# One encoder layer on one core: the softmax denominators turned into columns, the first loads reordered, the last norm taken into the feed-forward stage

## The chip, the cores and the metric

One core of one Trainium2 chip. The metric is the device time of one launch in microseconds; the median of the runs of the kernel before is 2854.69 us (2854.2 to 2859.28, three runs).

## What is computed

A transformer-like layer on two sequences of 512 and 1024 tokens (1536 tokens, twelve tiles of 128), model width 1024, all in float32:

```python
h = rmsnorm(x, norm_mix_pre); z = h @ w_in
a_out = axial_gqa(aq, ak, av, q_norm, k_norm) @ w_attn_o     # 8 query heads, 2 key heads, head width 64
m_out = bidir_mlstm(mq, mk, mv, mo, gates, ...) @ w_mlstm_o  # 4 heads of 128, both directions
x = x + rmsnorm((sigmoid(ga) * a_out + sigmoid(gm) * m_out) @ w_out, norm_mix_post)
u = rmsnorm(x, norm_ffn_pre) @ w_up
y = (gelu(conv3(u[..., :2816])) * u[..., 2816:]) @ w_down
return x + rmsnorm(y, norm_ffn_post)
```

In the attention the scores of a head are exp(q.k - top), the probabilities are weighted with v, and the result is divided by the sum of the probabilities. q and k are normed per head with one gain of 64 numbers for queries and one for keys.

## The kernel before, in words

Every product is made of three float32r products (high and low parts of both operands, `mm3`, L75). The engines' programs are written out by hand, each engine runs its list in order, and they meet at semaphores. The stages follow each other behind barriers: `norm_and_qkv`, `attention`, `mlstm`, `mlstm_norm`, `merge`, `out_projection`, `ffn`, `final_norm`.

**`norm_and_qkv`**, for each of twelve tiles of tokens: ScalarE takes the squares and the root (`statistics`), VectorE scales (`scale`), TensorE turns (`turn_x`), both keep high and low parts (`keep_hi`, `keep_lo`), TensorE projects (`project`). The weights come in eight slices of 128 x 784; VectorE makes the high part and the low part of each (`split_w`: a cast, L268, and a subtraction, L270). `raw` holds four slices, so slice 4 is asked for when slice 0 is split. Before ScalarE takes its first square it issues, on its own queue, the load of `mix_gain`, ten loads of head gains (one for each of the ten heads, a row of 64 numbers sent to 128 partitions) and the tables `cos` and `sin`.

**`attention`** works on 24 units: a key head, a chunk of 512 queries, a query head. A unit has 4 or 8 tiles of keys and takes 2 or 4 steps, 80 steps in all, each step two tiles of keys. The engines run over slots, one step each, with the work of several steps in one slot: at slot i TensorE does a part of the projection that fills the gaps (`project`, 384 units of three matmuls), `turn_top` of the unit that starts at slot i+3, `weigh(i)`, more of the projection, `scores(i+2)`, `sums` of the unit that ended at slot i-1, and the `piece`s. ScalarE does `exp(i+1)` and `keep_hi(i+1)`, VectorE `keep_lo(i+1)`, then `invert` and `normalise`, `fold`, the projection's low parts, `reduce` of the pieces, `top` and `add_halves`. GpSimd adds up the probabilities (`p_sum`, L723).

A `piece` is a 128 x 512 block of scores, made only for its row maximum; VectorE reduces it out of PSUM (`pM`, two banks). `turn_top` turns the four columns of maxima into a row in PSUM (`pD`, one bank, L944), and ScalarE copies it beside the queries (`keep_top`). `sums` multiplies a 128 x 128 matrix of ones with the folded probabilities, so that all 128 rows of the same bank `pD` hold the 512 denominators (L976, L977); `invert` takes the reciprocal of 64 x 512 of them into `att_rinv` (L842), and `normalise` multiplies (L849). Because `pD` is used by both, TensorE's program waits in front of `turn_top`:

```python
                for u in starting(i + 3):
                    if sums_done:
                        pe.wait_ge(inverted, sums_done)
                    turn_top(u)
```

**`ffn`** goes over 22 blocks of 128 hidden units. For each block TensorE makes the gate (`pG`) and the value (`pVal`), ScalarE and VectorE the convolution, the gelu and the split activation (`activate`), TensorE twelve tiles x two halves of the down projection, and VectorE adds each half to `y_sum` (`add_down`, L2072). The last block's `down_products` waits for all three chunks of the activation.

**`final_norm`** is a stage of its own: for each tile ScalarE takes the squares and the root, VectorE the reciprocal, the scaled product (L2245) and the sum with `x1` (L2250), SyncE stores the tile.

Of the kernel before, what the change touches and what calls it, by code (L numbers as in the profile page):

```python
# [30 lines left out]
P = 128  # L31
D = 1024
# [49 lines left out]
def norm_and_qkv(nc, k):  # L82

    with ExitStack() as ctx:
# [14 lines left out]
        qk_gain = sb("qk_gain", [P, NHEADS_QK, HEAD])  # L99
        cos = sb("cos", [P, NT, HEAD // 2])  # L100
# [44 lines left out]
        def _(sp):  # L145
# [30 lines left out]
            for kt in range(1, 4):  # L176
                load_w(kt)
            load_x(2)
# [17 lines left out]
        def _(act):  # L196
# [68 lines left out]
        def _(dve):  # L265
            def split_w(kt):
                dve.wait_ge(w_in[kt % 4], 32 * (kt // 4 + 1))
                dve.tensor_copy(wq_hi[:, kt, :], raw[:, kt % 4, :]).then_inc(w_hi_done, 1)  # L268
# [45 lines left out]
            split_w(0)  # L314
            dve.wait_ge(gain_in, 16)
            scale(0)
            split_w(1)
            scale(1)
            split_w(2)
            keep_lo(0)  # L320
# [5 lines left out]
            dve.wait_ge(const_in, 16 * (NHEADS_QK + 2))  # L326

            dve.tensor_scalar(qk_gain[:, 0:NQ, :], qk_gain[:, 0:NQ, :], Q_SCALE, None, ALU.mult).then_inc(gain_scaled, 1)
            dve.wait_ge(gain_scaled, 1)
# [11 lines left out]
        def _(pool):  # L341
            pool.wait_ge(const_in, 16 * (NHEADS_QK + 2))
# [182 lines left out]
def attention(nc, k):  # L525

    with ExitStack() as ctx:
# [35 lines left out]
        ones = sb("att_ones", [P, P], F32R)  # L563
# [4 lines left out]
        o_half, o_sum, o_out = sb("o_half", [H2, CH]), sb("o_sum", [H2, CH]), sb("o_out", [H2, 2, CH])  # L568
        top2, tops = sb("att_top2", [P, 4, 2]), sb("att_tops", [P, 4, P])
        rinv = sb("att_rinv", [H2, CH])  # L570
# [4 lines left out]
        g_ones = sb("gate_ones", [R, 2 * CH])  # L575
# [14 lines left out]
        summed, inverted, normed = sem("p_summed"), sem("inverted"), sem("o_normed")  # L590
# [24 lines left out]
        def pieces_until(i):  # L615
            return sum(len(x) for x in PIECES[:i + LEAD])

# [7 lines left out]
        def _(sp):  # L625
# [47 lines left out]
            for i in slots():  # L673
# [14 lines left out]
                for u in ending(i - 2):  # L688
# [37 lines left out]
        def _(act):  # L726
# [14 lines left out]
            def keep_top(u):  # L741
                act.wait_ge(m_turned, u + 1)
                act.wait_ge(q_in[u % 3], 48 * (u // 3 + 1))
                act.activation(q_m[H2:H2 + 1, u % 3, :], pD[H2:H2 + 1, :], ACT.Copy).then_inc(m_kept, 1)
# [50 lines left out]
        def _(dve):  # L795
            def reduce(u, p):
# [4 lines left out]
                if n == 1:  # L801
                    if u and p == 0:
                        dve.wait_ge(m_turned, u)
                    dve.tensor_reduce(tops[:, qb, H2:H2 + 1], pM[:, at % 2, :], AX_X, ALU.max).then_inc(reduced, 1)
                else:
                    dve.tensor_reduce(top2[:, qb, s:s + 1], pM[:, at % 2, :], AX_X, ALU.max).then_inc(reduced, 1)  # L806
# [25 lines left out]
            def add_halves(u):  # L832
                dve.wait_ge(halved, u + 1)
                if u:
                    dve.wait_ge(normed, u)
                dve.tensor_tensor(o_sum[:, :], pO[0:H2, :], o_half[:, :], ALU.add).then_inc(o_added, 1)

            def invert(u):
                dve.wait_ge(summed, u + 1)
                if u:  # L840
                    dve.wait_ge(normed, u)
                dve.reciprocal(rinv[:, :], pD[0:H2, :]).then_inc(inverted, 1)  # L842

            def normalise(u):
                dve.wait_ge(inverted, u + 1)
# [3 lines left out]
                dve.tensor_tensor(o_out[:, u % 2, :], o_sum[:, :], rinv[:, :], ALU.mult).then_inc(normed, 1)  # L849
# [1538 lines left out]
```

## Time and profile before

| | us |
|---|---|
| median of three runs (lowest, highest) | 2854.69 (2854.2, 2859.28) |
| profiled execution, its own time | 2859.45 |
| span of the profile, first to last instruction | 2857.6 |
| TensorE busy | 2483.2 (87%) |
| VectorE busy | 1786.3 (63%) |
| ScalarE busy | 885.8 (31%) |
| GpSimd busy | 497.1 (17%) |

The profile is of one execution. The shares are means over stages: by the turn of the attention's first piece at 199.1 us, of its last sums at 852.7 us, of the feed-forward stage's first product at 1729.1 us and its last sum's start at 2813.1 us, each stage has to be read by itself. Matmuls are pipelined: a 128 x 512 matmul is listed with 0.39 us, and the next starts 0.23 us after it.

### The profile page before, as it was taken

The numbers are of one execution on the slowest core, as the hardware profiler recorded it, in microseconds if no ns is written. First come the engines' busy times: TensorE is split into PE (matmuls) and PEld (weight loads), VectorE is DVE, ScalarE is ACT, GpSimd is POOL, SyncE is SP. The second block draws the span as 40 slices with busy tenths as digits, with TensorE's granted clock in tenths as the row PEclk, the third lists the DMA queues.
The fourth block names the chain that finished last, engine by engine and source line by source line (L and its number), as shares of the span: only waits on it lengthen the run. The fifth ranks groups of instructions, "written<-read, shape, count | busy, mean of one in ns | idle before, by whom it ended". The sixth has DMA issues, their size and how long they took to land. (4 is left out here: it accounts for less than half of the span.)

```text
span 2857.6 us, 32937 instructions
## 1 busy us (share of the span) xinstructions
PE 2483.2 (87%) x11024; PEld 2034.7 (71%) x11024; DVE 1786.3 (63%) x2308; ACT 885.8 (31%) x1395; POOL 497.1 (17%) x430
## 2 busy tenths in 40 slices
PE   5948778878886999997597988999999999999993
PEld 4836666657664878876485776888888888888882
DVE  4626777777764666665534553757576666656577
ACT  2314434434443554544410331111212111111113
POOL 1521222222323544443221000000000000000000
PEclk9968889989997999998798998999999999999996
DMA  6774224323217454532354431111101011111104
GB/s 179 200 195 119 80 70 132 104 69 116 81 54 223 115 177 116 158 96 88 128 182 147 138 116 52 38 29 35 31 22 42 24 37 29 37 29 37 29 15 184
DMA packets 286224, 268.20 MB, mean 94 GB/s; under 512 B 21672, under 2 KB 228776, under 8 KB 286128
## 3 DMA queue, kind: packets, MB, share of 16 engines
q1 hardware_dynamic: 281376, 253.18, 29.7%
q10 hardware_dynamic: 4752, 13.83, 1.2%
q8 instruction: 49, 0.80, 0.1%
q14 instruction: 47, 0.39, 0.0%
HBM read 197.70 MB, written 69.26 MB: 93 GB/s over the span
## 5 line engine op out<-in xcount | busy, mean ns | idle before, releaser
L2072 DVE TENSOR_TENSOR y_sum<-y_sum,pVal 128x512 f32<-128x512 f32 x252 | 171.5, 687 | 208.6 <-PE pVal L79 208.6
L77 PE MATMUL pG<-h2T_hi,wg_hi 128*128 128x512 f32 x528 | 206.5, 391 | 11.2 <-DVE wg_lo L2019 11.2
L78 PE MATMUL pG<-h2T_hi,wg_lo 128*128 128x512 f32 x528 | 206.3, 391 | 0.0
L79 PE MATMUL pG<-h2T_lo,wg_hi 128*128 128x512 f32 x528 | 206.3, 391 | 0.0
L77 PE MATMUL pVal<-h2T_hi,wv_hi 128*128 128x512 f32 x528 | 205.4, 389 | 0.0
L78 PE MATMUL pVal<-h2T_hi,wv_lo 128*128 128x512 f32 x528 | 205.4, 389 | 0.0
L79 PE MATMUL pVal<-h2T_lo,wv_hi 128*128 128x512 f32 x528 | 205.4, 389 | 0.0
L723 POOL TENSOR_TENSOR p_sum<-p_sum,probs 128x1024 f32<-128x1024 f32 x56 | 137.0, 2446 | 379.9 <-ACT probs L733 379.9
L1201 POOL TENSOR_TENSOR w_sum<-w_sum,w_all 128x512 f32<-128x512 f32 (+3 forms) x128 | 149.5, 1168 | 240.9 <-DVE w_all L1306 219.2
L77 PE MATMUL pZ_a<-hT_hi_a,win_hi_a 128*128 128x512 f32 x384 | 158.0, 412 | 31.5 <-DVE win_lo_a L497 27.6
L2117 ACT ACT_TABLE_LOAD x22 | 28.2, 1283 | 477.1 <-DVE conv L2052 477.1
L2072 DVE TENSOR_TENSOR y_sum<-y_sum,pD 128x512 f32<-128x512 f32 x252 | 172.3, 687 | 0.6 <-PE pD L79 0.6
L77 PE MATMUL pZ_m<-hT_hi_m,win_hi_m 128*128 128x512 f32 x384 | 159.4, 415 | 6.6 <-DVE win_lo_m L497 6.3
L78 PE MATMUL pZ_a<-hT_hi_a,win_lo_a 128*128 128x512 f32 x384 | 156.5, 407 | 0.0
L79 PE MATMUL pZ_a<-hT_lo_a,win_hi_a 128*128 128x512 f32 x384 | 155.5, 405 | 0.0
L78 PE MATMUL pZ_m<-hT_hi_m,win_lo_m 128*128 128x512 f32 x384 | 154.3, 402 | 0.0
L79 PE MATMUL pZ_m<-hT_lo_m,win_hi_m 128*128 128x512 f32 x384 | 153.9, 401 | 0.0
L806 DVE TENSOR_REDUCE att_top<-pM 128x1 f32<-128x512 f32 x128 | 86.7, 689 | 96.5 <-PE pM L938 96.5
L819 DVE TENSOR_TENSOR p_lo<-probs,p_hi 128x1024 fp32r<-128x1024 f32 x80 | 130.6, 1632 | 10.7 <-ACT p_hi L739 9.7
L733 ACT ACTIVATE probs<-pS 128x512 f32<-128x512 f32 x160 | 87.5, 595 | 156.3 <-PE pS L956 156.2
L497 DVE TENSOR_TENSOR win_lo_m<-win_raw_m,win_hi_m 128x1024 fp32r<-128x1024 f32 x48 | 67.5, 1406 | 97.4 <-ACT win_hi_m L493 97.4
L77 PEld LDWEIGHTS pG<-h2T_hi,wg_hi 128*128 128x128 f32 x528 | 99.8, 189 | 32.4 <-DVE wg_lo L2019 11.6
(260 smaller groups left out, 6272.4 us busy)
## 6 DMA issues: line engine op xcount, KB each, us to landing
win_raw_a<-in_w_in SPq DMA_DIRECT2D x48, 512.0 KB, 4.2
win_raw_m<-in_w_in SPq DMA_DIRECT2D x48, 512.0 KB, 4.2
ffn_raw<-in_w_up SPq DMA_DIRECT2D x44, 512.0 KB, 3.9
zT_scratch<-z_st_a SPq DMA_DIRECT2D x48, 256.0 KB, 4.4
zT_scratch<-z_st_m SPq DMA_DIRECT2D x48, 256.0 KB, 4.4
a_T<-zT_scratch SPq DMA_DIRECT2D x16, 768.0 KB, 8.6
ffn_raw<-in_w_down SPq DMA_DIRECT2D x22, 512.0 KB, 4.4
m_raw<-zT_scratch SPq DMA_DIRECT2D x36, 256.0 KB, 3.1
```

The lines of the kernel that those rows point to most:

```text
L77: pe.matmul(out, w_hi, x_hi, start=first, stop=False, **kw)
L78: pe.matmul(out, w_lo, x_hi, start=False, stop=False, **kw)
L79: return pe.matmul(out, w_hi, x_lo, start=False, stop=last, **kw)
L497: dve.tensor_tensor(self.w_lo[:, g % 2], self.raw[:, g % 2], self.w_hi[:, g % 2].bitcast(F32), ALU.subtract).then_inc(self.split, 1)
L723: pool.tensor_tensor(acc[:, u % 2, :], acc[:, u % 2, :], probs[:, i % 2, :], ALU.add).then_inc(added_up, 1)
L733: act.activation(probs[:, i % 2, a * CH:(a + 1) * CH], pS[:, a, :], ACT.Exp).then_inc(exped, 1)
L806: dve.tensor_reduce(top2[:, qb, s:s + 1], pM[:, at % 2, :], AX_X, ALU.max).then_inc(reduced, 1)
L819: dve.tensor_tensor(p_lo[:, i % 3, :], probs[:, i % 2, :], p_hi[:, i % 3, :].bitcast(F32), ALU.subtract).then_inc(lo_done, 1)
L1201: pool.tensor_tensor(w_sum[:, j % 2, d, cols], w_sum[:, j % 2, d, cols], w_all[:, x % RING, cols], ALU.add).then_inc(added_up, 1)
L2072: dve.tensor_tensor(y_sum[:, t, cols], y_sum[:, t, cols], down_bank(2 * t + h), ALU.add).then_inc(summed, 1)
L2117: act.activation(gelu[:, :], conv[:, :], ACT.Gelu_apprx_tanh, bias=b).then_inc(gelu_done, 1)
```

## The change

Three parts.

**Start.** The ten loads of head gains on ScalarE's queue become two (`head_gain`), and they, `cos` and `sin` go on SyncE's queue behind the first four weight slices; VectorE spreads the two gains over ten heads. The high parts of the weights are made by ScalarE (`w_high`) between its squares, VectorE keeps the subtraction.

**Attention.** The maxima are turned into a bank of `pM`, which they share with the pieces in the order `M_ORDER`; `wait_bank` waits for whoever held the bank two places before. `sums` takes the folded probabilities as the weights and two columns of ones as the moving side, four blocks x (high, low), so that the denominators of 128 queries stand in a column. `invert` takes the reciprocal of 128 x 4 and spreads it to 128 x 512 by a product with ones (`rwide`); `turn_inverse` turns that back into rows of `pD`; `normalise` multiplies straight out of `pD`. Each of these has a slot of its own: `sums` at one slot after the unit's end, `invert` and `turn_inverse` at two, `normalise` and the store at three. `o_sum` has two buffers.

**End.** `final_norm` goes; in `ffn` the last block's down projection goes tile by tile through two pairs of banks and starts with the first chunk of the activation, VectorE adds a whole tile at once (`last_sum`), ScalarE takes the squares, VectorE scales two tiles later (`scale`), GpSimd adds `x1`, SyncE stores. `x1` is loaded into the place of `h2_hi` during the last block's value products.

```diff
@@ norm_and_qkv
+            sp.dma_start(cos[:, :, :], k.cos).then_inc(const_in, 16)
+            sp.dma_start(sin[:, :, :], k.sin).then_inc(const_in, 16)
+            for g, src in enumerate((k.q_norm, k.k_norm)):
+                sp.dma_start(head_gain[:, g, :], src.partition_broadcast(P)).then_inc(const_in, 16)
             load_x(2)
...
+            def w_high(kt):
+                act.wait_ge(w_in[kt % 4], 32 * (kt // 4 + 1))
+                act.activation(wq_hi[:, kt, :], raw[:, kt % 4, :], ACT.Copy).then_inc(w_hi_done, 1)
...
-            for h in range(NHEADS_QK):
-                g = k.q_norm if h < NQ else k.k_norm
-                act.dma_start(qk_gain[:, h, :], g.partition_broadcast(P)).then_inc(const_in, 16)
-            act.dma_start(cos[:, :, :], k.cos).then_inc(const_in, 16)
-            act.dma_start(sin[:, :, :], k.sin).then_inc(const_in, 16)
             statistics(0)
+            w_high(0)
             statistics(1)
+            w_high(1)
             keep_hi(0)
+            w_high(2)
+            w_high(3)
             keep_hi(1)
+            for kt in range(4, KD):
+                w_high(kt)
@@ attention
+        def wait_bank(pe, m):
+
+            if m >= 2:
+                kind, n = M_ORDER[m - 2]
+                pe.wait_ge(m_kept if kind == "turn" else reduced, n + 1)
...
             def invert(u):
                 dve.wait_ge(summed, u + 1)
+                dve.reciprocal(rinv[:, :], pD[:, 0:8].rearrange("p (q e) -> p q e", e=2)[:, :, 0]).then_inc(inverted, 1)
+                dve.wait_ge(inverted, u + 1)
                 if u:
-                    dve.wait_ge(normed, u)
-                dve.reciprocal(rinv[:, :], pD[0:H2, :]).then_inc(inverted, 1)
+                    dve.wait_ge(r_turned, u)
+                dve.tensor_tensor(rwide[:, :, :], wide_ones, rinv[:, :].unsqueeze(2).to_broadcast([P, 4, P]),
+                                  ALU.mult).then_inc(widened, 1)
...
-                dve.tensor_tensor(o_out[:, u % 2, :], o_sum[:, :], rinv[:, :], ALU.mult).then_inc(normed, 1)
+                dve.tensor_tensor(o_out[:, u % 2, :], o_sum[:, u % 2, :], pD[0:H2, :], ALU.mult).then_inc(normed, 1)
...
             def sums(u):
                 pe.wait_ge(fold_split, u + 1)
-                pe.matmul(pD[:, :], ones[:, :], s_hi[:, :], start=True, stop=False)
-                pe.matmul(pD[:, :], ones[:, :], s_lo[:, :], start=False, stop=True).then_inc(summed, 1)
+                if u:
+                    pe.wait_ge(normed, u)
+                for qb in range(4):
+                    cols = slice(qb * P, (qb + 1) * P)
+                    pe.matmul(pD[:, 2 * qb:2 * qb + 2], s_hi[:, cols], ones[:, :], start=True, stop=False)
+                    last = pe.matmul(pD[:, 2 * qb:2 * qb + 2], s_lo[:, cols], ones[:, :], start=False, stop=True)
+                last.then_inc(summed, 1)
+
+            def turn_inverse(u):
+                pe.wait_ge(widened, u + 1)
+                for qb in range(4):
+                    last = pe.transpose(pD[:, qb * P:(qb + 1) * P], rwide[:, qb, :], k.ident[:, :])
+                last.then_inc(r_turned, 1)
...
                 for u in starting(i + 3):
-                    if sums_done:
-                        pe.wait_ge(inverted, sums_done)
                     turn_top(u)
...
                 for u in ending(i - 1):
-                    pe.wait_ge(m_kept, tops_done)
                     sums(u)
-                    sums_done += 1
+                for u in ending(i - 2):
+                    turn_inverse(u)
@@ ffn
+                pool.tensor_tensor(row, row, x_row(t), ALU.add).then_inc(added, 1)
...
+            dve.wait_ge(post_in, 16)
+            for t in range(NT + 2):
+                if t < NT:
+                    last_sum(t)
+                if t >= 2:
+                    scale(t - 2)
...
-            down_products(last_f)
...
+                pe.wait_ge(act_l, NCH * last_f + t // 4 + 2)
+                if t >= 2:
+                    pe.wait_ge(done_t, t - 1)
```

## Rows read from the trace of the kernel before

**Rows 1.** Busy time of all engines in the attention: PE, PEld, DVE, ACT, POOL, PEclk, DMA.

```profile
216.00:853.00 637.00, 519.52 (x2074) 411.00 (x2072) 469.97 (x452) 280.15 (x390) 161.90 (x80) 0.90 0.32 92
```

**Rows 2.** Waits within the attention, 216 to 853 us: total, times, longest.

```profile
PE pDen L944 <- DVE att_rinv L842: 89.6, 20, 6.9
...
PE pO L969 <- DVE o_sum L836: 11.0, 6, 5.4
```

**Rows 3.** VectorE's groups over the span: busy, mean ns | idle before.

```profile
L842 DVE RECIPROCAL att_rinv<-pDen 64x512 f32<-64x512 f32 x24 | 80.2, 3342 | 0.5 <-PE pDen L977 0.5
...
L830 DVE TENSOR_TENSOR p_fold_lo<-p_fold,p_fold_hi 128x512 fp32r<-128x512 f32 x24 | 16.6, 692 | 0.8
```

**Rows 4.** VectorE in order of time, around one of these waits: start, us.

```profile
504.72 0.85 DVE L815 TENSOR_TENSOR att_tops<-att_top 128x4 f32<-128x4 f32 x1
...
508.30 3.34 DVE L842 RECIPROCAL att_rinv<-pDen 64x512 f32<-64x512 f32 x1
```

**Rows 5.** TensorE in order of time, behind the same wait.

```profile
511.69 1.11 PE L944 MATMUL pDen<-ident,att_tops 128*128 128x128 f32 x4 [6.35 <-DVE att_rinv L842]
...
513.46 0.63 PE L969 MATMUL pO<-p_hi,v_both 128*128 128x512 f32 x1
513.88 0.63 PE L970 MATMUL pO<-p_lo,v_both 128*128 128x512 f32 x1
...
515.90 0.39 PE L956 MATMUL pS<-q_max,k_low 65*128 65x512 f32 x1
516.13 0.39 PE L955 MATMUL pS<-q_stack,k_stack 128*128 128x512 f32 x1
```

**Rows 6.** TensorE in order of time: eight transposes in the first stage.

```profile
44.96 1.03 PE L374 MATMUL pT<-ident,x_scaled 128*128 128x128 f32 x8
```

**Rows 7.** TensorE in order of time: sixteen two-column matmuls of the mLSTM stage.

```profile
920.53 0.25 PE L1439 MATMUL pMV<-m_ones,w_sum_lo 128*128 128x2 f32 x1
920.64 0.25 PE L1438 MATMUL pMV<-m_ones,w_sum_hi 128*128 128x2 f32 x1
...
922.01 0.35 PE L1438 MATMUL pMV<-m_ones,w_sum_hi 128*128 128x2 f32 x1
922.23 0.35 PE L1439 MATMUL pMV<-m_ones,w_sum_lo 128*128 128x2 f32 x1
```

**Rows 8.** GpSimd in order of time, two of its sums.

```profile
517.58 2.40 POOL L723 TENSOR_TENSOR p_sum<-p_sum,probs 128x1024 f32<-128x1024 f32 x1 [12.04 <-ACT probs L733]
...
527.90 2.62 POOL L723 TENSOR_TENSOR p_sum<-p_sum,probs 128x1024 f32<-128x1024 f32 x1 [3.82 <-ACT probs L733]
```

**Rows 9.** VectorE in order of time, beside these sums.

```profile
518.63 2.44 DVE L819 TENSOR_TENSOR p_lo<-probs,p_hi 128x1024 fp32r<-128x1024 f32 x1 [0.21 <-ACT p_hi L739]
...
524.10 1.23 DVE L819 TENSOR_TENSOR p_lo<-probs,p_hi 128x1024 fp32r<-128x1024 f32 x1 [0.19 <-ACT p_hi L739]
...
528.77 0.67 DVE L836 TENSOR_TENSOR o_sum<-pO,o_half 64x512 f32<-64x512 f32 x1
```

**Rows 10.** All engines and queues in order of time, at the start.

```profile
3.22 6.92 ACTq L246 DMA_DIRECT2D qk_gain<-in_q_norm  x8
...
19.58 1.28 ACT L202 ACT_TABLE_LOAD   x1 [19.58 <-issue]
...
40.10 0.97 DVE L270 TENSOR_TENSOR wqkv_lo<-wqkv_raw,wqkv_hi 128x784 fp32r<-128x784 f32 x1
```

**Rows 11.** The loads of x_t, from issue to landing.

```profile
DMA to landing us min/median/max: 4.1/4.9/9.5
```

**Rows 12.** VectorE in order of time, at the end.

```profile
2794.71 0.69 DVE L2059 TENSOR_TENSOR act_lo<-gelu,act_hi 128x512 fp32r<-128x512 f32 x1 [0.70 <-ACT act_hi L2120]
...
2821.00 1.28 DVE L2245 SCALAR_TENSOR_TENSOR f_y<-y_sum,f_stat,f_gain 128x1024 f32<-128x1024 f32 x1 [0.24 <-DVE f_stat L2242]
...
2853.27 1.23 DVE L2250 TENSOR_TENSOR f_y<-f_y,f_x 128x1024 f32<-128x1024 f32 x1
```

**Rows 13.** ScalarE in order of time, the first square of the last stage.

```profile
2816.42 1.28 ACT L2226 ACT_TABLE_LOAD   x1 [21.73 <-PEq L2263]
```

More of the change, by code:

```diff
@@ L893, in _ @@
                     invert(u)
+                for u in ending(i - 3):
                     normalise(u)
@@ L1012, in _ @@
             sums(NU - 1)
+            turn_inverse(NU - 1)
             pe.wait_ge(exped, 2 * NS)
@@ L1973, in ffn, with halves, x_row, pair @@
         last_f = NFF - 1
+        def halves(a):
+            return a.rearrange("p (h n) -> p h n", n=CH)
+        def x_row(t):
+            return h2_hi[:, 2 * (t % XR):2 * (t % XR) + 2, 0:CH].bitcast(F32)
+        def pair(t):
+            return pG[:, 0:2, :] if t % 2 == 0 else pD[:, :, :]
         def down_bank(j):
@@ L2003, in _, with load_x1 @@
                 three(2 * i + 1, 1)
+            def load_x1(t):
+                sp.dma_start(x_row(t), halves(k.x1[t * P:(t + 1) * P, :])).then_inc(x_in[t % XR], 16)
+            sp.dma_start(post[:, :], k.norm_ffn_post.partition_broadcast(P)).then_inc(post_in, 16)
+            sp.wait_ge(vald, NCH * last_f + 2)
+            for t in range(XR):
+                load_x1(t)
+            for t in range(NT):
+                sp.wait_ge(added, t + 1)
+                sp.dma_start(k.y[t * P:(t + 1) * P, :], y_sum[:, t, :]).then_inc(y_out, 16)
+                if t + XR < NT:
+                    load_x1(t + XR)
+            sp.wait_ge(y_out, 16 * NT)
+        @block.gpsimd
+        def _(pool):
+            for t in range(NT):
+                pool.wait_ge(scaled, t + 1)
+                pool.wait_ge(x_in[t % XR], 16 * (t // XR + 1))
+                row = halves(y_sum[:, t, :])
+                pool.tensor_tensor(row, row, x_row(t), ALU.add).then_inc(added, 1)
         @block.vector
@@ L2097, in _, with last_sum, scale @@
             step(NFF // 2 - 1, 1, last=True)
-            add_down(last_f)
+            def last_sum(t):
+                dve.wait_ge(downed, NDT * last_f + t + 2)
+                dve.wait_ge(summed, NDT * last_f + 1)
+                row = halves(y_sum[:, t, :])
+                dve.tensor_tensor(row, row, pair(t), ALU.add).then_inc(done_t, 1)
+            def scale(t):
+                dve.wait_ge(rooted, t + 1)
+                dve.reciprocal(stat[:, 2, t:t + 1], stat[:, 1, t:t + 1]).then_inc(inverted, 1)
+                dve.wait_ge(inverted, t + 1)
+                dve.scalar_tensor_tensor(out=y_sum[:, t, :], in0=y_sum[:, t, :], scalar=stat[:, 2, t:t + 1],
+                                         in1=post[:, :], op0=ALU.mult, op1=ALU.mult).then_inc(scaled, 1)
+            dve.wait_ge(post_in, 16)
[4 more added lines that the diff above has]
+                    scale(t - 2)
         @block.scalar
@@ L2124, in _ @@
                 gelus(f)
+            act.wait_ge(wsplit, 3 * NFF + 1)
+            for t in range(NT):
+                act.wait_ge(done_t, t + 1)
+                if t:
+                    act.wait_ge(squared, t)
+                act.activation(raw[:, 0, :], y_sum[:, t, :], ACT.Square,
+                               accum_out=stat[:, 0, t:t + 1]).then_inc(squared, 1)
+                act.wait_ge(squared, t + 1)
+                act.activation(stat[:, 1, t:t + 1], stat[:, 0, t:t + 1], ACT.Sqrt, scale=1.0 / D,
+                               bias=k.eps[:, 0:1]).then_inc(rooted, 1)
         @block.tensor
@@ new lines, in _ @@
+            pe.wait_ge(wsplit, 3 * last_f + 4)
+            pe.wait_ge(gate_copied, NCH * NFF + 1)
+            for t in range(NT):
+                pe.wait_ge(act_l, NCH * last_f + t // 4 + 2)
+                if t >= 2:
+                    pe.wait_ge(done_t, t - 1)
+                else:
+                    pe.wait_ge(summed, NDT * last_f + 1)
+                for h in range(D // CH):
+                    cols = slice(h * CH, (h + 1) * CH)
+                    last = mm3(pe, pair(t)[:, h, :], act_hi[:, t * P:(t + 1) * P], act_lo[:, t * P:(t + 1) * P],
+                               d_hi[:, cols], d_lo[:, cols], True, True)
+                last.then_inc(downed, 1)
```

140 lines of the change are left out of this document (46 added, 94 removed).

## The prediction

> **What bounds the kernel now.** I read the page first: TensorE is busy in 87% of the span, so the question is where it is not, or where it is slow. The table of windows by stage puts the loss in the attention: 637 us from 216 to 853, of which TensorE is busy in about 519 [rows 1]. The list of waits in that stretch [rows 2] names the cause of most of the other 117: 20 waits of TensorE in front of L944, `turn_top`, for the reciprocal `att_rinv`, 89.6 us in all. Next to it stand 11.0 us for `o_sum` and some 17 us for all the rest (117 - 89.6 - 11.0). The groups of VectorE [rows 3] give the other side: 24 reciprocals of 64 x 512 take 3.34 us each, 80.2 us.
>
> Is the reciprocal really what TensorE needs there? The timeline of VectorE around one wait [rows 4] shows that it isn't: the maxima that `turn_top` turns are complete at 504.72 + 0.85 = 505.57, and the reciprocal begins only at 508.30 and ends at 511.64. The timeline of TensorE [rows 5] shows the transposes starting at 511.69 after 6.35 us idle, so it had been ready since 505.34. It waited 6.35 us for a bank and would have waited about 0.3 us for its data. I made the same comparison for all 20 waits (the last matmul's end, the last `top` or `reduce` before the transposes): of 89.6 us the data would have cost some 2.4. A first wait of 4.5 us, without a reciprocal, stays.
>
> The second thing in [rows 5] is what the wait leaves behind. The matmuls after it start 0.42 us apart (513.46, 513.88), some eight in a row, and only at 515.90 the distance is 0.23 again (515.90, 516.13). That is the lower of the granted clock's two levels, 1.2 instead of 2.4 GHz, after an idle engine; the stage's mean granted clock is 0.90 [rows 1]. One such stretch costs 8 x (0.42 - 0.23) = 1.5 us on matmuls and about 0.3 on the four transposes, 1.8 us.
>
> At the two ends other things bound: at the start the data, at the end VectorE.
>
> **The change, part by part.**
>
> *Attention, the waits.* With the maxima in `pM`, `turn_top` waits for its data and for a bank whose last user was a piece already reduced (`top` comes behind it). Gain 89.6 - 2.4 = 87 us. With them the slow stretches go: 20 x 1.8 = 36 us; bounds 0, if the clock falls for another reason, and 36. As the second piece after a turn now waits for ScalarE's `keep_top`: ScalarE is busy for 280 of 637 us [rows 1] and has nothing between the turn and that copy, so I put nothing; without that cover it is one copy, some 0.6 us by two thirds, 10 us over 24 units.
>
> *Attention, work added on TensorE.* `turn_inverse` is four transposes; eight at the full clock take about 1.0 us [rows 6], so four add 0.45. `sums` becomes eight two-column matmuls; in the mLSTM stage such matmuls start 0.11 us apart at the full clock and 0.22 at the lower one [rows 7]; eight are 0.9 us, against two of 0.23 before, so +0.44. Together 0.9 x 24 = +21 us, all of it on the engine that bounds.
>
> *Attention, VectorE.* The reciprocal of 128 x 4 costs a few tenths at most (I take 0.2: next to a whole 64 x 512 in 3.34 it has 1/128 of the columns, and the rest is what an instruction costs at least); `rwide` is a 128 x 512 product of two operands in SBUF like L830, 0.69 [rows 3]. So each unit gives back 3.34 - 0.9 = 2.45 us, 59 us of VectorE's 470 [rows 1]. None of it counts by itself. VectorE was busy 470 of 637, 74%; it will be busy about 411 in some 550 us, 75%, so it keeps its slack.
>
> *Attention, waits added.* TensorE waits for `rwide` in front of `turn_inverse`, and for `normalise` of the unit before in front of `sums`. Behind them on TensorE stand the pieces, a third of the projection and the next slot, for which ScalarE's exp and VectorE's reduce wait. `turn_inverse` stands after the transposes, weigh's four matmuls, three of the projection and four of the scores, 3 us later in the slot than the old wait; VectorE comes 3.34 - 0.9 = 2.4 us earlier. The old wait was 4.5 us in the mean (89.6 / 20), 4.5 - 5.4 is below zero, so on the mean it's hidden; for the spread I put 0.2 us a unit, 5 us. `sums` behind `normalise` matters only for the eight units of two steps, where it comes in the same slot; I put it with the rest: the 28 us that TensorE already waits for other things in this stage may grow when the slots get shorter, and I add somewhat under half of them, 12 us. Bounds for these two: 0, and 24 x 2 = 48 us if each unit finds VectorE late by one blocked instruction (next paragraph but one).
>
> At the stage's end the last `att_rinv` stands alone between the last sums and the store (0.5 us idle before it [rows 3]); 3.34 becomes 0.2 + 0.7 + 0.45 and handovers: -2 us. Sum of the stage: -87 - 36 + 21 + 5 + 12 - 2 = -87 us; bounds -125 (no waits added, everything recovered) and -40 (waits added in full, half the clock).
>
> *Start.* ScalarE's first square waits for nothing but its own queue, which issues twelve loads from 3.22 on and comes to the table load at 19.58 [rows 10]. The first `x` is asked for before 3.22 and lands 4.1 to 9.5, mostly 4.9 us later [rows 11], thus at about 8. So the first square moves by 19.58 - 8 = 11.5 us (7 to 12.5). From there to the last split of the weights at 40.10 + 0.97 [rows 10] the chain goes over VectorE's scale, TensorE's transposes and the splits; the casts leave VectorE and stand on ScalarE, which otherwise waits for transposes there, so I let the chain have its length or a little less: -12 us, bounds -7 and -15. `cos`, `sin` and two gains are now four issues on SyncE's queue in front of `load_x(2)` and the fifth weight slice; both wait for the first scale and split anyway, which come later than four issues.
>
> *End.* Now: the last activation is ready at 2794.71 + 0.69 = 2795.4 [rows 12], and the span ends at 2857.6, 62 us later. Then: VectorE's first `last_sum` can't start before 2795.4, as it stands behind `activate` on its engine; TensorE has two tiles done by then. 1.2 us for a tile (L2250's 1.23 for 128 x 1024 [rows 12]), then ScalarE's first square and root with their table loads and the reciprocal, 2821.00 - 2816.42 = 4.6 us [rows 12, 13], then the first scaled product, 1.28: 2802.5. From there eleven more tiles. On VectorE alone a tile is 1.2 + 0.3 + 1.3 = 2.85, and the last two have no `last_sum` left. But GpSimd adds `x1`, two operands in SBUF, and its sum of 128 x 1024 takes 2.40 [rows 8]. What this does to VectorE is seen in [rows 8, 9]: `p_lo`, two operands in SBUF, started at 518.63 beside a sum of GpSimd that ended at 519.98, and took 2.44 instead of the 1.23 of the one at 524.10, that is it ended 1.09 after GpSimd; `o_sum` at 528.77, one operand in PSUM, took 0.67 in the midst of another such sum. So `last_sum` goes beside GpSimd, and `scale` (the tile and the gain, both SBUF) doesn't: a tile takes 2.40 + 1.1 + 0.1 = 3.6 us. Eleven are 40 us: the last `scale` ends at 2842, the last addition at 2845, and the store needs 3.1 us as now (2853.27 + 1.23 to 2857.6): 2848, a gain of 9 us. Without such blocking it's 2802.5 + 9 x 2.85 + 2 x 1.6 + 2.4 + 3.1 = 2837, a gain of 21 us.
> The Trainium skill, page SBUF — State Buffer, section SBUF: two separate sides, says that VectorE and GpSimd share a port pair that one instruction holds for its whole length, a VectorE instruction with two SBUF inputs among them, while the other is fully blocked. By it the end gives 9 us as I take it; were it a sharing of the bandwidth, it would lie between 9 and 21. The trace agrees for `p_lo`; no row shows it for `scalar_tensor_tensor`.
>
> Sum: -87 - 12 - 9 = -108 us against the profiled execution's 2859.45 (span 2857.6): 2751. That execution is 4.8 us above the median of the runs, 2854.69; from the median it's 2746, which I predict.
>
> **The rivals.**
> 1. *Likeliest, as summed up: 2746*, its own range 2726 to 2766. For it: the data of `turn_top` are there in [rows 4]; at full pace between waits the slots go on without TensorE waiting for VectorE.
> 2. *The wait comes back in pieces.* VectorE's slot holds blocked `p_lo`s (2.44 instead of 1.23), and shorter slots bring GpSimd's sums nearer together; if TensorE waits 2 us more a unit, at `turn_inverse`, the pieces or the weighing, the stage gives 40 instead of 87: 2793. Against it: VectorE's 75%.
> 3. *The clock falls at the narrow sums.* In [rows 7] the matmuls go from 0.11 to 0.22 apart within sixteen narrow ones: the clock fell with TensorE issuing. Eight narrow ones a unit could do the same: 24 x 1.8 = 43 us: 2789. Against it: here scores stand before and pieces behind, and there are eight.
> 4. *No blocking at the end*, and the start at its bound: 12 + 3 us more gain: 2731.
> 5. *The change doesn't do what it says*: `turn_top` waits as long for its bank in `pM`, because `keep_top` or the reduces before are late. The stage then pays 21 us for nothing and the ends give 21: 2855, no change.
> 6. *Slower.* The wait moves to `turn_inverse` whole: each unit, `rwide` stands behind a `p_lo` that GpSimd blocks and is blocked by the next sum itself. It decides from a wait of (108 + 6) / 24 = 4.8 us a unit on; at 6 us, two blocked instructions and a slow clock behind them, the time is 2746 + 24 x 6 = 2890. Against it: TensorE comes there 3 us later than at the old wait and VectorE 2.4 earlier.
>
> **How the numbers follow.** Chances: first 0.54, second 0.21, third 0.08, fourth 0.11, fifth 0.03, sixth 0.03. The time is the first's. The range 2718 to 2796 takes in the second to the fourth with the bounds of start and end; outside stay the last two and the far ends of the others. A measurement of this kernel tells changes over about 0.2% (5.7 us) from none: faster 0.94 (the first four), same 0.03 (the fifth), slower 0.03.
>
> **What would show it.** After the change: L842 gone from VectorE, two short groups in its place (0.2 and 0.7 us); no wait of TensorE in front of the transposes of `att_tops` over 1 us; the attention some 550 us long with a granted clock near 0.95; the first square at about 9 us instead of 20; in the last stage `scale` instructions of 1.3 to 3.5 us that end 1.1 us after GpSimd's additions, and a tile every 3.6 us. The prediction is wrong if TensorE's idle time shows up in front of `turn_inverse`, `sums` or the pieces with more than 1 us a unit, or if the matmuls after `sums` start 0.42 us apart.

## The result, and the profile after

The kernel after takes 2712.74 us (median of 4 runs, 2709.49 to 2717.91), the kernel before on the same chip 2856.99 (4 runs, 2854.2 to 2862.86): the ratio is 0.9494, 95% interval 0.9471 to 0.9518, about 144 us less. The forecast was 2746, with a range from 2718 to 2796: the direction was right, the gain was larger than the range allowed. The profiled execution of the kernel after took 2717.91 us, its span is 2716.1.

Where the time went, by the first instruction of each stage in the two traces:

| from ... to | before, us | after, us | difference | forecast |
|---|---|---|---|---|
| start to the attention's first load of `q_stack` | 184.8 | 167.6 | -17.2 | -12 |
| from there to the mLSTM's first load of `m_raw` | 679.9 | 560.1 | -119.8 | -87 |
| from there to the end of the last `act_lo` | 1930.7 | 1938.6 | +7.9 | 0 |
| from there to the end of the span | 62.2 | 49.8 | -12.4 | -9 |

So the attention holds most of the error. Its row in the windows (the window and its length, then the columns of [rows 1]: busy time of each engine with its number of instructions, granted clock, DMA share and GB/s):

```profile
198.00:718.00 520.00, 502.09 (x2309) 404.78 (x2308) 395.54 (x476) 280.65 (x390) 163.95 (x80) 0.99 0.39 112
```

TensorE was idle for 637 - 519.5 = 117.5 us before [rows 1] and is idle for 17.9 now; its busy time fell by 17 us although it has more matmuls, as the granted clock rose from 0.90 to 0.99. Nearly nothing is left to gain from waits in this stage. The waits of TensorE in the same stretch (total, times, longest; all that are over 1 us; `DVEq` is VectorE's queue, which here signals without an instruction that a unit's maxima are ready):

```profile
PE pO L1004 <- DVE o_sum L867: 5.4, 4, 4.1
...
PE pZ_a L77 <- DMA hT_lo_a<-hT_lo_scratch: 4.1, 6, 1.7
...
PE pM L979 <- DVEq L842: 3.1, 1, 3.1
...
PE pDen L1022 <- DVE att_rwide L875: 1.9, 3, 0.9
...
PE pDen L1015 <- DVE o_out L883: 1.1, 1, 1.1
```

The 89.6 us for `att_rinv` [rows 2] are gone, and the two new waits, for `att_rwide` (L1022, `turn_inverse`) and for `o_out` (L1015, `sums`), come to 3 us. The surprise is in the old ones. The wait for `o_sum`, 11.0 before [rows 2], has halved, and one of the kernel before that the forecast counted in "the rest" is down to 0.2 us. In the kernel before it was

```profile
PE pZ_a L77 <- DVE win_lo_a L497: 7.6, 3, 4.5
```

The forecast had these old waits growing by 12 us. (`win_lo_a` is the low part of the weights of the projection that fills the gaps; the expectations below call it the window's low part, or `w_low`.) What VectorE does for the new chain, from its groups in the stage (busy, mean ns | idle before):

```profile
L875 DVE TENSOR_TENSOR att_rwide<-gate_ones,att_rinv 128x512 f32<-128x512 f32 x23 | 15.9, 692 | 0.8
L883 DVE TENSOR_TENSOR o_out<-o_sum,pDen 64x512 f32<-64x512 f32 x23 | 15.4, 670 | 0.0
...
L871 DVE RECIPROCAL att_rinv<-pDen 128x4 f32<-128x4 f32 x24 | 4.1, 172 | 0.9 <-PE pDen L1016 0.9
```

At the end of the kernel, in order of time on VectorE and GpSimd (start, duration; L2197 is `scale`, L2091 GpSimd's addition):

```profile
2670.59 1.28 DVE L2197 SCALAR_TENSOR_TENSOR y_sum<-y_sum,f_stat,f_gain 128x1024 f32<-128x1024 f32 x1
...
2671.95 2.38 POOL L2091 TENSOR_TENSOR y_sum<-y_sum,h2T_hi 128x1024 f32<-128x1024 f32 x1 [1260.09 <-DVE y_sum L2197]
...
2673.11 2.31 DVE L2197 SCALAR_TENSOR_TENSOR y_sum<-y_sum,f_stat,f_gain 128x1024 f32<-128x1024 f32 x1
...
2675.49 2.38 POOL L2091 TENSOR_TENSOR y_sum<-y_sum,h2T_hi 128x1024 f32<-128x1024 f32 x1 [1.16 <-DVE y_sum L2197]
...
2676.66 2.30 DVE L2197 SCALAR_TENSOR_TENSOR y_sum<-y_sum,f_stat,f_gain 128x1024 f32<-128x1024 f32 x1
```

The first `scale` runs alone and takes 1.28 us. The second starts beside an addition that ends at 2671.95 + 2.38 = 2674.33 and itself ends at 2675.42, 1.09 later; the next addition starts when it has ended. The two engines take turns, and a tile takes 2676.66 - 2673.11 = 3.55 us.

And the start, ScalarE in order of time (L207 is the square of the statistics):

```profile
3.23 1.28 ACT L207 ACT_TABLE_LOAD   x1 [3.23 <-PEq L2330]
8.02 1.06 ACT L207 ACTIVATE x_scaled<-x_t 128x1024 f32<-128x1024 f32 x1 [3.51 <-DMA x_t<-in_x]
```

The table load is done long before `x` lands, and the first square starts with its data at 8.02 (it began at 20.88 before, behind the table load of [rows 10]).

### The profile page after: what moved, and what is told of

Its sections match the earlier page's. It is cut to its first block and busy times, and to the rows that moved or that the text cites. A ratio compares the mean times of both kernels' runs of the same rounds, so it can differ in the third digit from the quotient of the medians.

```text
span 2716.1 us, 33252 instructions
## 1 busy us (share of the span) xinstructions
PE 2469.5 (91%) x11264; PEld 2030.7 (75%) x11264; DVE 1701.6 (63%) x2301; ACT 886.9 (33%) x1398; POOL 527.4 (19%) x442
## 5 line engine op out<-in xcount | busy, mean ns | idle before, releaser
L2160 DVE TENSOR_TENSOR y_sum<-y_sum,pVal 128x512 f32<-128x512 f32 x240 | 163.4, 688 | 205.8 <-PE pVal L79 205.8
L2091 POOL TENSOR_TENSOR y_sum<-y_sum,h2T_hi 128x1024 f32<-128x1024 f32 x12 | 28.4, 2362 | 1272.9 <-DVE y_sum L2197 1272.9
L2160 DVE TENSOR_TENSOR y_sum<-y_sum,pD 128x512 f32<-128x512 f32 x240 | 164.2, 688 | 0.0
L850 DVE TENSOR_TENSOR p_lo<-probs,p_hi 128x1024 fp32r<-128x1024 f32 x80 | 127.5, 1594 | 10.4 <-ACT p_hi L770 9.4
L837 DVE TENSOR_REDUCE att_top<-pM 128x1 f32<-128x512 f32 x128 | 86.6, 689 | 75.7 <-PE pM L972 74.6
```

Source lines behind the costliest of these rows:

```text
L837: dve.tensor_reduce(top2[:, qb, s:s + 1], pM[:, piece_bank(at), :], AX_X, ALU.max).then_inc(reduced, 1)
L850: dve.tensor_tensor(p_lo[:, i % 3, :], probs[:, i % 2, :], p_hi[:, i % 3, :].bitcast(F32), ALU.subtract).then_inc(lo_done, 1)
L2091: pool.tensor_tensor(row, row, x_row(t), ALU.add).then_inc(added, 1)
L2160: dve.tensor_tensor(y_sum[:, t, cols], y_sum[:, t, cols], down_bank(2 * t + h), ALU.add).then_inc(summed, 1)
```

## The experiments

Times are medians. Differences from before go by the ratio to the kernel before timed beside each, differences from after are those of the medians.

| kernel | us | ratio to before, 95% interval | attention (`q_stack` to `m_raw`), us |
|---|---|---|---|
| before | 2857 to 2861 | 1 | 679.9 |
| after | 2712.74 | 0.9471 to 0.9518 | 560.1 |
| start only | 2844.99 | 0.9936 to 0.9961 | 679.1 |
| loads of the start only | 2845.97 | 0.9942 to 0.9968 | 680.0 |
| attention only | 2742.12 | 0.9575 to 0.9617 | 563.2 |
| end only | 2847.35 | 0.9938 to 0.9964 | 681.0 |
| own bank, long reciprocal | 2813.98 | 0.9815 to 0.9862 | 632.1 |
| shared bank, short reciprocal | 2773.23 | 0.9678 to 0.9711 | 588.4 |
| own bank, short reciprocal | 2728.78 | 0.9519 to 0.9550 | 544.2 |
| after, chain in two slots | 2760.96 | 0.9624 to 0.9674 | 609.1 |
| after, dead reciprocals in a row | 2789.92 | 0.9735 to 0.9781 | 635.8 |
| after, dead reciprocals spread | 2749.91 | 0.9595 to 0.9627 | 599.9 |
| after, gain in PSUM | 2700.00 | 0.9429 to 0.9453 | 559.7 |
| power on GpSimd | 4541.94 | 1.5842 to 1.5895 | - |

**The three parts alone.** The hunks of the diff, sorted by stage.

> The kernel before with the attention's part of the change alone (maxima through pM's ring, narrow sums, reciprocal of 128x4, spread and turned back); the start and the end are those of before. If the parts simply add up, as the comparison of the two traces has them (start -17, attention -120, end -12, middle stages +8), this kernel takes about 2857 - 120 = 2737 us, and 2745 us if the middle stages' +8 us is caused by the attention's stage; TensorE's waits in the attention are those of the kernel after (about 18 us of idle time). If a part of the attention's gain came from the start (other phase of the loads or the clock), it is 2750 us or more.

> The kernel before with the start's part of the change alone. The comparison of the two traces has -17 us up to the attention's first load (forecast -12): 2840 us if it is carried to the end unchanged; 2845 us if only the forecast -12 is; 2857 us if the attention takes it back.

> The kernel before with the end's part of the change alone (post norm and residual row by row, with GpSimd's add and the loads inside the last stage). The comparison of the traces has -12 us behind the last low part of the activations: 2845 us if it stands by itself; 2848 us by the forecast of -9. The middle stages as in before: if the +8 us of the kernel after in them is scatter of the clock, they are as in before here too.

By their ratios they give -115.5, -14.9 and -14.0 us, in sum -144.4; the whole change gives -144.5. The parts add up within their intervals (some 6 us either way for the attention, 4 for each end), so no part needs another to work. The 7.9 us lost in the middle belong to none: from the first load of `m_raw` to the first product of the last stage it is 864.4 us in the profile of before and 872.7 in that of after, but over the profiles of the other kernels, whose code there is the same, the values lie anywhere between (865.8 with the attention's part alone, 870.3 with the end's alone, and 866.2 with the gain in PSUM, whose stages up to there are those of after). I take it as scatter from execution to execution.

**Loads or casts at the start.** The start's part without the move of the casts: loads reordered, head gains once per kind, but VectorE still makes the high parts, in its old order.

> The kernel before with the loads' part of the start alone: the head gains come once per kind and on SyncE's queue with cos and sin, VectorE spreads them; the high parts of the weights stay on VectorE and the order of its work is that of before. If ScalarE's queue of 13 loads ahead of its table load was the whole cost (the first square comes 12.9 us earlier after), this takes 2840 to 2845 us, within 4 us of start_only. If the casts' move to ScalarE carries part of it (12 casts of 1.2 us less on VectorE, 15 us), it takes 2848 to 2853 us, 8 us or more above start_only.

2845.97 against 2844.99: the loads are most of it. What moving the casts gives, the medians can't tell, as the intervals overlap, but the traces do: VectorE ends the last split of the weights at 40.10 + 0.97 = 41.07 us before [rows 10], at 28.55 with the loads alone and at 25.70 with the whole start, so the loads give 12.5 us there and the casts 2.9. (The expectation's price for the casts was wrong: they are eight of 0.56 us, not twelve of 1.2.)

**Bank or length.** The change takes two things away at once: the maxima no longer share `pD` with the chain, and the reciprocal is short. The first alone, on the kernel before:

```
-    last = pe.transpose(pD[:, qb * P:(qb + 1) * P], tops[:, qb, :], k.ident[:, :])
+    last = pe.transpose(pM[:, turn_bank(u), qb * P:(qb + 1) * P], tops[:, qb, :], k.ident[:, :])
...
     def sums(u):
         pe.wait_ge(fold_split, u + 1)
+        if u:
+            pe.wait_ge(inverted, u)
```

> The kernel before with one thing changed: the maxima are turned through pM's ring instead of pD; the wide sums, the 64x512 reciprocal of 3.34 us and the single o_sum stay. Theory A (the prediction's own): the wait for pD was what the old order cost, and the reciprocal's length on VectorE is hidden: the 89.6 us of waits go, and the 28 us of other waits stay as they are or grow: 2765 to 2775 us. Theory B: the 3.34 us reciprocal also stands in VectorE's queue ahead of p_lo, the window's low parts and the sum of the halves, and the other waits that halved in the kernel after (o_sum 11.0 to 5.4, w_low 7.6 to 0.2) halved because it went: then this kernel keeps the o_sum and w_low waits at 11 and 7 us or more, and loses 15 to 40 us against attention_only (2755 to 2780 us, with those waits seen). Theory C: without the wait the rest follows by itself, whatever the reciprocal's length: within 10 us of attention_only, with the o_sum and w_low waits down too.

It came out at 2814, outside all three: only some 46 us gained, so theory A falls, and theory B comes nearest, with the waits that it named and too small a size. The stage's row and waits:

```profile
213.00:805.00 592.00, 511.79 (x2100) 401.79 (x2099) 480.00 (x453) 280.74 (x390) 165.10 (x80) 0.93 0.35 99
```
```profile
PE pO L988 <- DVE o_sum L855: 30.2, 10, 5.5
...
PE pZ_a L77 <- DVE win_lo_a L497: 27.8, 14, 4.6
...
PE pM L956 <- DVE att_top L825: 10.8, 2, 6.3
```

The wait for the bank is gone, and TensorE is still idle for 80 us: it now waits for other work in VectorE's queue, 69 us in these three groups. One such place, VectorE in order of time, then TensorE:

```profile
504.53 3.34 DVE L861 RECIPROCAL att_rinv<-pDen 64x512 f32<-64x512 f32 x1
507.91 2.55 DVE L868 TENSOR_TENSOR o_out<-o_sum,att_rinv 64x512 f32<-64x512 f32 x1
510.38 1.21 DVE L497 TENSOR_TENSOR win_lo_a<-win_raw_a,win_hi_a 128x1024 fp32r<-128x1024 f32 x1
```
```profile
507.52 0.39 PE L956 MATMUL pM<-k_stack,q_stack 128*128 128x512 f32 x1
511.64 0.79 PE L77 MATMUL pZ_a<-hT_hi_a,win_hi_a 128*128 128x512 f32 x1 [3.73 <-DVE win_lo_a L497]
```

TensorE is done at 507.91 and needs `win_lo_a`, which does not depend on the chain at all. VectorE gets to it at 510.38, after 3.34 us of reciprocal and a 2.55 us product behind it, and TensorE starts 0.05 us after it has ended. The product takes 0.68 us where it runs alone. Here, with both operands in SBUF, it stood beside one of GpSimd's sums and ended 0.55 us after it:

```profile
507.56 2.35 POOL L742 TENSOR_TENSOR p_sum<-p_sum,probs 128x1024 f32<-128x1024 f32 x1 [4.03 <-ACT probs L752]
```

Over the stage the 24 products take 35.8 us in this kernel and 16.4 in the one with both causes gone (below), while `p_lo` takes 112.1 here and 132.0 there: when an instruction's turn comes also decides whether GpSimd holds it up.

The second alone, on the kernel before, with 64 of the 512 columns inverted (0.54 us):

```
-    dve.reciprocal(rinv[:, :], pD[0:H2, :]).then_inc(inverted, 1)
+    dve.reciprocal(rinv[:, 0:H2], pD[0:H2, 0:H2]).then_inc(inverted, 1)
```

> The kernel before with one thing changed: the reciprocal takes 64 of its 512 columns (the others are left at 1, so part of the computation is left out), about 0.45 us instead of 3.34; the maxima stay in pD, sums and normalise stay as before. It is the fourth cell of a square whose others are before (shared bank, long: 2857), bank_only (own bank, long: 2814) and attention_only (own bank, short: 2742). Theory B (the reciprocal's length in VectorE's queue is the larger part): each of the 20 waits for pD shrinks by 2.9 us and the waits behind a late VectorE go: -60 to -85 us, 2775 to 2800 us. Theory A (the shared bank is what counts): the maxima still wait for the reciprocal's turn in the queue, 2820 us or more.

2773: -87 us with the bank shared as before, even a little more than theory B gave. The waits in the stage:

```profile
PE pDen L945 <- DVE att_rinv L842: 35.2, 18, 4.1
...
PE pO L970 <- DVE o_sum L836: 9.2, 6, 4.1
...
PE pZ_a L77 <- DVE win_lo_a L497: 0.2, 1, 0.2
```

The wait for the bank falls from 89.6 to 35.2 with the bank still shared. The fourth cell has both:

> bank_only with the reciprocal of 64 columns as in short_only (part of the computation is left out), so both causes are gone and TensorE has neither the narrow sums nor the transposes back. Against attention_only it shows what the added work on TensorE costs: if TensorE bounds the stage (502 us busy of 520 after), it is the 21 us forecast: 2742 - 21 = 2721 us; if that work is hidden, 2735 to 2742 us.

2728.78: between the two numbers expected. By the length of the stage the square reads 680 (neither), 632 (own bank, -48), 588 (short, -92) and 544 (both, -136): the two nearly add up (-140), and the reciprocal's length is two thirds of it. The wait for `win_lo_a` goes with the length: it is 0.2 us in both kernels with the short reciprocal. The halved wait for `o_sum` does not, as the fourth cell shows:

```profile
PE pO L989 <- DVE o_sum L855: 10.2, 8, 4.1
```

It is 5.4 only with the attention's part as it was written, so the halving belongs to something else in that part, the second buffer of `o_sum` or the slots of the chain; which, no run shows.

The attention's part as it was written takes 563 us, 19 more than the fourth cell. That is the price of the narrow sums and the transposes back, less what the shorter waits give: TensorE is busy for 481.1 us of this kernel's stage and for 503.8 with the attention's part, 22.8 more, and idle for 23.4 and 19.2.

**Is it VectorE's total, or the run of long work?** After plus dead work behind each `normalise`, which nothing reads:

```
+    for n in range(2):
...
+        dve.reciprocal(idle_r[:, :], g_ones[0:H2, 0:CH // 2]).then_inc(idled, 1)
```

> The kernel after, with dead work added: two reciprocals of 64x256 (together about 3.3 us, as long as the old one of 64x512) on VectorE behind each of the 24 normalise steps; nothing waits for their result. It adds 80 us of VectorE's time to the attention's stage (about 405 to 485 us of 520). Theory A (length hidden, only the place in the chain counted): within 8 us of after, up to 2721 us. Theory B (the long instruction delays what is queued behind it): +15 to +40 us, 2728 to 2753 us, and the waits for o_sum and w_low come back to 11 and 7 us.

And about the same amount in 80 pieces, one at the end of each step:

> The kernel after with as much dead work on VectorE as in long_reciprocal_load (83 us there, +77 us of time), but in 80 pieces of 64x152 (about 1.04 us each), one at the end of each step, instead of 3.5 us in a row at each of 24 units' ends. If it is the run of long instructions at the unit's end that makes p_lo and the sum of the halves late, most of it is hidden in VectorE's 120 us of idle time: 2713 to 2735 us. If VectorE's total counts, it costs as much as before: 2775 to 2795 us.

48 x 1.74 = 84 us of dead work cost 77 us in a row (2789.92) and 80 x 1.08 = 87 us cost 37 spread out (2749.91); the stage is longer by 75.7 and 39.8 us. The waits, of the first and of the second kernel:

```profile
PE pO L1010 <- DVE o_sum L869: 31.7, 11, 5.9
...
PE pZ_a L77 <- DVE win_lo_a L507: 13.9, 8, 3.8
```
```profile
PE pO L1010 <- DVE o_sum L869: 22.9, 14, 5.2
...
PE pDen L1028 <- DVE att_rwide L877: 9.9, 5, 3.8
```

With nothing shared and nobody waiting for it, the long work brings the same two waits as in the kernel with its own bank. The row of the first kernel's stage shows where its price lies:

```profile
200.00:794.00 594.00, 530.36 (x2310) 422.24 (x2308) 479.71 (x523) 280.88 (x390) 168.48 (x80) 0.94 0.35 99
```

TensorE is idle for 63.6 us where it was idle for 17.9 after, and busy for 28 us more on as many matmuls, at a granted clock of 0.94 instead of 0.99.

Both theories were too low for the first kernel; for the second the truth lies between. The same amount of work costs half as much when it does not stand in a row. How the 37 us divide between VectorE's total and the pieces that still stand in a crowded slot is not shown, and the comparison is not quite clean: the 80 `p_lo` take 99.1 us in the spread kernel, where 10 of them overlap one of GpSimd's sums, but 125.6 with the dead work in a row (41 of them) and 127.5 after (47). So VectorE's busy time in the stage grew by 68 us in the spread kernel (395.5 to 463.3) and by 84 in the other.

**A slot per step of the chain.** After, with `normalise` and `store_a` back in the slot of `invert`:

```
-                for u in ending(i - 3):
                     normalise(u)
```

> The kernel after, with normalise and the store back in the slot of the reciprocal (slot i-2 instead of i-3). normalise then waits on VectorE for the transposes that TensorE issues later in the same slot. If the slot per step matters, VectorE's queue stands for each of the 23 units by the time from the spread's end to the transposes' end (2 to 5 us), p_lo and the maxima come late, and the kernel takes 20 to 90 us more than after (2735 to 2800 us). If VectorE's idle time (some 50 us of waits for products in this stage) covers it, it is within 5 us of 2713.

2760.96, 48 us more than after: the slot matters. VectorE waits for the transposes, and what is queued behind it is late, `o_sum` once more:

```profile
DVE o_out L883 <- PE pDen L1021: 48.2, 23, 5.0
...
PE pO L1003 <- DVE o_sum L867: 21.9, 9, 4.6
```

**The turns at the end.** After, with ScalarE copying the post-norm's gain to two free PSUM banks:

```
+    act.activation(pV[:, 0:2, :], halves(post[:, :]), ACT.Copy).then_inc(post_kept, 1)
...
-    in1=post[:, :], op0=ALU.mult, op1=ALU.mult).then_inc(scaled, 1)
+    in1=pV[:, 0:2, :], op0=ALU.mult, op1=ALU.mult).then_inc(scaled, 1)
```

> The kernel after with one operand moved: ScalarE copies the post-norm's gain into two free PSUM banks, and the scaling on VectorE reads it there instead of in SBUF. In the kernel after the scaling ends about 1.1 us after GpSimd's add of the row before, whatever it started at (2.27 to 2.31 us beside an add, period 3.53 us a row). If the two operands in SBUF are what GpSimd holds up, the scaling runs beside the add and the period falls to that of VectorE or GpSimd alone (2.4 to 2.9 us): 16 rows save 10 to 18 us, 2695 to 2703 us. If the result or the single operand in SBUF is enough to be held up, the period stays and the time is 2711 to 2715 us.

2700.00 us, the fastest kernel of this study, 13 below after; 11 of them lie behind the last `act_lo` (38.7 us to the end of the span instead of 49.8). The rows are twelve, not the expectation's sixteen. VectorE and GpSimd in order of time:

```profile
2668.45 1.28 DVE L2199 SCALAR_TENSOR_TENSOR y_sum<-y_sum,f_stat,pVal 128x1024 f32<-128x1024 f32 x1
...
2670.97 1.28 DVE L2199 SCALAR_TENSOR_TENSOR y_sum<-y_sum,f_stat,pVal 128x1024 f32<-128x1024 f32 x1
```
```profile
2669.81 12.47 POOL L2092 TENSOR_TENSOR y_sum<-y_sum,h2T_hi 128x1024 f32<-128x1024 f32 x5
```

Each `scale` takes its 1.28 us in the midst of GpSimd's additions, which go on without a pause (12.47 for five, 2.49 each), and a tile takes 2670.97 - 2668.45 = 2.52 us instead of 3.55.

**The reciprocal on another engine.** A try at saving the 19 us on TensorE too: maxima in `pM`, wide sums, and GpSimd raising the 64 x 512 denominators to the power -1.

> A try at a better attention on the kernel before: maxima in pM's ring as after, wide sums as before, but the reciprocal leaves VectorE: ScalarE copies the 64 rows of pD to SBUF (about 0.6 us), and GpSimd raises them to the power -1 there; normalise and store stand two steps later. No work is added on TensorE. If GpSimd needs 3 to 8 us for 64x512, it has the room (164 us busy of 520) and the kernel takes attention_only less TensorE's added work: 2715 to 2735 us. If it needs more than about 13 us a unit, p_sum comes late and it takes more than 2800 us.

4541.94 us. The instruction takes 82.5 us, 24 times:

```profile
L739 POOL TENSOR_TENSOR att_rinv<-att_rinv,att_minus x24: 81920/82502/83981, 250.1 to 2451.3; 64x512 f32<-64x512 f32 x24
```

## Why the prediction was right and wrong

**The step that failed** is the sentence on VectorE's gain in the attention: "None of it counts by itself", because VectorE, busy for 74% of the stage, "keeps its slack". With it go the terms that it led to: "the 28 us that TensorE already waits for other things in this stage may grow", +12, and the 5 for `turn_inverse`. By these terms TensorE was to stay idle for 117.5 - 87 + 17 = 47.5 us of the stage; it is idle for 17.9, and these 30 us are nearly the whole error of 33. The new waits came to 3 us instead of 17, with a slot for each step of the chain (with two slots for it the kernel takes 48 us more). The old ones did not grow but shrank by 13: 7.4 for `win_lo_a`, which went with the reciprocal's length, and 5.6 for `o_sum`, whose cause is open. What the runs show in place of the failed step is that VectorE's time counts: the short reciprocal alone gave 92 of the stage's 136 us, and dead work of its length cost 77 us for 84. VectorE's idle time stands where it waits for TensorE's products, in the kernel before above all here:

```profile
DVE att_top L806 <- PE pM L938: 96.5, 90, 5.5
```

In the slots behind a unit's last step `p_lo`, the reciprocal and its product, the fold, the projection's low part, the maxima and the sum of the halves are queued in this order (all in one slot for the units of two steps), and TensorE needs several of them next. In the place shown above for the kernel with its own bank, VectorE works from 504.53 to 511.59 without a pause while TensorE waits. A mean share of busy time said nothing about such a place.

**The reading of the 89.6 us** as a wait for a bank and not for data was right, and yet it attributed too much to the bank. The wait ended with the reciprocal, so it could be shortened at either end: with its own bank the maxima no longer waited, but TensorE stood for 69 us in three other groups of waits for VectorE (18.6 in two of them before); with a short reciprocal the same wait fell to 35.2 with the bank still shared. The forecast's -87 for the waits and -36 for the clock needed both. That these two sizes came true is in part luck: the prediction put them down to the bank, which alone shortens the stage by 48 us, and had no price for the shorter reciprocal that gave the rest.

**The sum of the attention**, -87, missed -120 by 33. The measured value lies within the bounds of -125 and -40 only because -125 leaves out the +21 of work added on TensorE, which no shorter wait takes away. With it the best case in the prediction's own terms is -87 - 36 + 21 - 2 = -104, and the stage went 16 us beyond that, most of it by the old waits, for whose shrinking the sum has no term. The term for the clock was right: on as many matmuls as before, TensorE is busy for 481.1 us in the fourth cell against 519.5, 38 less (forecast 36). So was the work added on TensorE, +21: 22.8 us of busy time, 19 of the stage's length.

**Start**: -12, bounds -7 and -15; alone it measured -14.9 (11 to 18 by the interval), in the profile -17.2. Some 2 us of the latter are scatter: six other profiles with the start of before reach the first load of `q_stack` at 182.4 to 183.1 us, the profile of before at 184.8. The first square came at 8.02, forecast about 9, as the table load of 1.28 us is done while the data are under way. The other 2.9 us are the casts, for which the forecast took nothing off the chain, or "a little".

**End**: -9, bounds 9 to 21 of gain; measured -14 alone and -12.4 in the profile. The mechanism stood as written: `scale` ends 1.09 us after GpSimd's addition, a tile takes 3.55 us (3.6 in the forecast). The first `scale` ended 5.5 us behind the last `act_lo`, 7.1 in the forecast, and the eleven tiles after it took 38.8 us instead of 40. The Trainium skill, page SBUF — State Buffer, section SBUF: two separate sides, has VectorE and GpSimd take an exclusive lock on a shared port pair, on VectorE's side for an instruction with two inputs in SBUF beside a GpSimd instruction that reads SBUF. This case agrees, for `scalar_tensor_tensor` as well: 2.31 us with the gain in SBUF, 1.28 with it in PSUM, beside the same additions. So rival 4, no blocking at the end, was wrong for this kernel, but its period (2.85) could be had by moving one operand, and then was 2.52.

**Rivals 2, 5 and 6** fell with the waits: `turn_inverse` waits for 1.9 us in all, `turn_top` for 3.6, of which 3.1 is its first wait. Of rival 2 the mechanism is real, only it worked the other way: TensorE does wait behind VectorE's long instructions, and the change made the longest of them short. **Rival 3** fell too: eight narrow sums are 0.11 us apart and the matmuls after them stay at the full pace (433.23, then 433.54 and 433.77; the granted clock of the stage is 0.99):

```profile
433.11 0.25 PE L1016 MATMUL pDen<-att_ones,p_fold_lo 128*128 128x2 f32 x1
433.23 0.48 PE L972 MATMUL pM<-k_stack,q_stack 128*128 128x512 f32 x1
433.54 0.40 PE L77 MATMUL pZ_a<-hT_hi_a,win_hi_a 128*128 128x512 f32 x1
433.77 0.40 PE L78 MATMUL pZ_a<-hT_hi_a,win_lo_a 128*128 128x512 f32 x1
```

**What stays open**: which piece of the attention's part halves the wait for `o_sum`, and how the 37 us of the spread dead work divide between VectorE's total and its place in the queue.

## What to carry to other kernels

When a wait ends with a long instruction, price both ways out of it: what the waiting engine would do without the wait, and what else is queued behind that instruction on its own engine. A low mean share of busy time is no slack; look at the stretch in which the other engine needs several results of the same queue, and put short instructions there, a step of a chain in each slot, so that none of them waits in the queue. Where VectorE and GpSimd work side by side on tiles in SBUF, look for one operand of VectorE's that can lie in PSUM.

## What the runs showed of the hardware

The reciprocal's time on VectorE goes by its columns: 3.34 us for 64 x 512, 1.74 for 64 x 256, 1.08 for 64 x 152, 0.54 for 64 x 64 and 0.17 for 128 x 4. Inverting 128 x 4 and spreading it (0.69) costs VectorE 0.86 us where the wide form costs 3.34. On TensorE the four transposes take 0.41 us from their start to that of the next matmul (439.50 to 439.91) and the eight narrow sums 0.81 (432.42 to 433.23), where the two wide sums took 0.47 (502.17 to 502.64 before). GpSimd's power takes 82.5 us for 64 x 512, some 25 times VectorE's reciprocal. Small products with two operands in SBUF are held up beside GpSimd's sums too: `o_out` of 64 x 512 took 0.68 us at its shortest and 2.55 beside the sum from 507.56 to 509.91 in the kernel with its own bank. With one operand in PSUM it stays at 0.67 in the kernel after, but none of its 24 runs stands beside a sum there, so that case is not shown.
